# Two phases per weight chunk: the products with its hi part first, then those with its lo part

## The reference

```python
z = rms_norm(h, mix_norm_gain[i]) @ w_in[i]                        # 2048 x 2112
h = h + jnp.concatenate([y_pool, y_mla], axis=-1) @ w_out[i]
q = (xn @ w_pq)                                                    # in peer()
act = jax.nn.gelu(jnp.einsum('tkd,td->tk', expert_u[ib], xb))      # rows gathered by index
return jnp.einsum('tk,tkd->td', act * gb, expert_v[ib])
proj = h @ w_in                                                    # second block, 2048 x 11264
return x + merged @ w_out
```

## Time and profile before

| | |
|---|---|
| median of 3 runs | 2645.71 us (2640.82 to 2649.74) |
| the profiled execution | 2644.75 us, its span 2643.3 us |
| mean granted clock of TensorE | 0.955 of full speed |
| busy, share of the span | PE 80%, DVE 54%, ACT 24%, POOL 25% |
| products | 7418 instructions on PE |
| HBM read | 747.84 MB, of which 207.63 MB over the queue of SP and its like, the rest gathered rows |

### The profile page before, as it was taken

How to read it: one execution, slowest core, us unless ns; L and a number is a source line. 1 busy time by engine, 2 the same in 40 slices (tenths; PEclk the granted TensorE clock), 3 DMA queues, 4 the chain that set the end, 5 groups by cost and what they waited for, 6 DMA issues and landing times.

```text
span 2643.3 us, 18981 instructions
## 1 busy us (share of the span) xinstructions
PE 2125.3 (80%) x7418; PEld 1361.2 (51%) x7418; DVE 1432.7 (54%) x1772; ACT 645.3 (24%) x857; POOL 648.1 (25%) x522
## 2 busy tenths in 40 slices
PE   7988887444777777777777777777999999999998
PEld 6876666331222222222222222224778778788887
DVE  4456457777667644444444444454554565654453
ACT  4244342121000000000000000012443353543342
POOL 0000001324554554445444554440000000000000
PEclk9988888767999999999999999999999999999999
DMA  5433246667999999999999999995545544455554
GB/s 215 158 119 117 86 177 222 240 237 311 422 421 421 422 421 422 422 422 421 422 422 421 422 421 422 421 422 225 175 161 194 204 141 154 173 176 191 191 188 146
DMA packets 104488, 751.19 MB, mean 284 GB/s; under 512 B 11856, under 2 KB 11856, under 8 KB 13264
## 3 DMA queue, kind: packets, MB, share of 16 engines
q0 software_dynamic: 73728, 536.90, 49.3%
q1 hardware_dynamic: 28512, 207.63, 22.4%
q10 hardware_dynamic: 2160, 5.45, 0.5%
HBM read 747.84 MB, written 2.10 MB: 284 GB/s over the span
## 4 chain that ended last, share of the span: by engine, by line
PE 44%; DMA 35%; DVE 12%; ACT 4%; issue 3%; POOL 2%; ACTq 0%; SPq 0%; POOLq 0%; DVEq 0%
DMA xT_rows<-in_expert_v,idx 26%; PE ps L278 11%; PE ps L279 11%; PE ps L280 11%; PE ps L512 8%; DMA W<-in_expert_u,idx 6%; DVE wlo L1038 3%; DMA xT_rows<-in_expert_u,idx 2%; DVE W L1339 2%; ACT whi L667 2%; POOL W L243 1%; POOL xT_rows L243 1%; PE ps L305 1%; DMA W<-in_expert_v,idx 1%; DVE W L1423 1%
## 5 line engine op out<-in xcount | busy, mean ns | idle before, releaser
L1038 DVE TENSOR_TENSOR wlo<-raw,whi 128x2048 fp32r<-128x2048 f32 x195 | 446.1, 2290 | 369.4 <-ACT whi L667 369.3
L278 PE MATMUL ps<-whi,xT 128*128 128x512 f32 (+1 forms) x1432 | 575.7, 402 | 85.8 <-DVE wlo L1038 82.9
L512 PE MATMUL ps<-xT_rows,W 128*128 128x512 f32 x960 | 448.0, 609 | 205.6 <-DMA xT_rows<-in_expert_v,idx 200.3
L279 PE MATMUL ps<-wlo,xT 128*128 128x512 f32 (+1 forms) x1432 | 568.2, 397 | 0.0
L280 PE MATMUL ps<-whi,xT 128*128 128x512 f32 (+1 forms) x1432 | 566.8, 396 | 0.0
L512 PE MATMUL ps<-W 128*128 128x512 f32 x960 | 442.3, 602 | 152.0 <-DMA W<-in_expert_v,idx 145.6
L667 ACT ACTIVATE whi<-raw 128x2048 fp32r<-128x2048 f32 x195 | 372.6, 1913 | 488.8 <-PE ps L280 470.4
L512 PEld LDWEIGHTS ps<-xT_rows,W 128*128 128x128 f32 x960 | 174.2, 192 | 478.7 <-issue 274.5
L1423 DVE CUSTOM_DVE_ANT_0 W<-W 128x2048 f32<-128x2048 f32 x112 | 256.4, 2292 | 265.2 <-DMA W<-in_expert_u,idx 264.7
L1423 DVE CUSTOM_DVE_ANT_0 xT_rows<-xT_rows,W 128x2048 f32<-128x2048 f32 x112 | 256.4, 2292 | 260.1 <-DMA xT_rows<-in_expert_u,idx 259.9
L512 PEld LDWEIGHTS ps<-W 128*128 128x128 f32 x960 | 172.0, 189 | 422.0 <-issue 236.0
(11 more groups left out here) (236 smaller groups left out, 1152.9 us busy)
## 6 DMA issues: line engine op xcount, KB each, us to landing
raw<-in_weights SPq DMA_DIRECT2D x196, 1024.0 KB, 4.9
W<-in_expert_u,idx POOLq DMA_INDIRECT x144, 16.4
h<-in_x SPq DMA_DIRECT2D x2, 1024.0 KB, 6.9
xT_rows<-in_expert_v,idx POOLq DMA_INDIRECT x128, 15.8
W<-in_expert_v,idx POOLq DMA_INDIRECT x128, 15.8
out<-h ACTq DMA_DIRECT2D x8, 256.0 KB, 4.7
xT_rows<-in_expert_u,idx POOLq DMA_INDIRECT x112, 16.4
W<-in_pool_op ACTq DMA_DIRECT2D x1, 1024.0 KB, 15.7
```

Of the source, the lines that this page charges most:

```text
L278: pe.matmul(o, a[0], b[0], start=start, stop=False)
L279: pe.matmul(o, a[0], b[1], start=False, stop=False)
L512: m = pe.matmul(ps[:, (4 if t == 0 else 0) + b, :], diag[:, i % DIAGS, :], slots[n % GR][:, b * NC:(b + 1) * NC], start=(unit % NH == 0 an ...
L1038: v.tensor_tensor(lo, raw[:, c % RAW, :], hi.bitcast(F32), ALU.subtract).then_inc(sem["lo_done"], 1)
```

## The change

Each chunk's products are issued in two phases. First the sixteen with the hi part of the weights (x_hi w_hi and x_lo w_hi), after a wait for `hi_done` only; the sixteenth raises a new semaphore, `hi_used`. Then, after a wait for `lo_done`, the eight with the lo part (x_hi w_lo); the last raises `used` as before. ScalarE's split of chunk c waits for `hi_used` of the chunk that was in the same `whi` slot, and for its `lo_done` (VectorE reads `whi` to make the lo part). VectorE's split gets a second wait, `used` of the chunk that was in the same `wlo` slot. `SPLIT_BEFORE[c]` is that chunk: c - 2, except where that would be C_KEYS, whose parts lie elsewhere: for c = 43 it is 39. `HI_USED` turns a chunk's number into the count of `hi_used`, which the four chunks outside `block_step` do not raise; where one of these was in the slot, ScalarE waits for `used` as before. The chunk of the rope columns (64 columns wide, 96 products) is treated in the same way, 64 and 32. The order within the first phase is for each slice and tile hi, then lo part of the activations; the sums in PSUM are made of the same terms in another order.

```diff
+OTHER_CHUNKS = (C_POOL, C_KEYS, C_PROJ, C_PROJ + 1)
+SPLIT_BEFORE = [c - 2 * SPL if c - SPL == C_KEYS else c - SPL for c in range(CHUNKS)]
+HI_USED = [sum(b not in OTHER_CHUNKS for b in range(c + 1)) for c in range(CHUNKS)]
...
-                pe.wait_ge(sem["lo_done"], c + 1)
                 hi, lo = whi[:, c % SPL, :], wlo[:, c % SPL, :]
                 nk = 4 if cols_n == NC else DK
+
+                def product(k, t, x, w_, start, stop):
+                    s = slice(t * 128, (t + 1) * 128)
+                    cs = slice(k * cols_n, (k + 1) * cols_n)
+                    return pe.matmul(ps[:, banks_of(b) + t, 0:cols_n], x[:, q0 + qn * 4 + k, s], w_[:, cs], start=start, stop=stop)
+
+                pe.wait_ge(sem["hi_done"], c + 1)
                 for k in range(nk):
                     for t in range(NT):
-                        s = slice(t * 128, (t + 1) * 128)
-                        cs = slice(k * cols_n, (k + 1) * cols_n)
-                        ks = q0 + qn * 4 + k
-                        m = matmul3(ps[:, banks_of(b) + t, 0:cols_n], (lh[:, ks, s], ll[:, ks, s]), (hi[:, cs], lo[:, cs]),
-                                    start=(qn == 0 and k == 0), stop=(qn == n_q - 1 and k == nk - 1))
+                        product(k, t, lh, hi, qn == 0 and k == 0, False)
+                        m = product(k, t, ll, hi, False, False)
+                m.then_inc(sem["hi_used"], 1)
+                pe.wait_ge(sem["lo_done"], c + 1)
+                for k in range(nk):
+                    for t in range(NT):
+                        m = product(k, t, lh, lo, False, qn == n_q - 1 and k == nk - 1)
                 m.then_inc(sem["used"], 1)
...
             def split(c):
                 a.wait_ge(landed[c % RAW], 16 * (c // RAW + 1))
                 if c >= SPL and c != C_KEYS:
-                    a.wait_ge(sem["used"], c - SPL + 1)
+                    if SPLIT_BEFORE[c] in OTHER_CHUNKS:
+                        a.wait_ge(sem["used"], SPLIT_BEFORE[c] + 1)
+                    else:
+                        a.wait_ge(sem["hi_used"], HI_USED[SPLIT_BEFORE[c]])
+                        a.wait_ge(sem["lo_done"], SPLIT_BEFORE[c] + 1)
                 a.activation(split_into(c)[0], raw[:, c % RAW, :], ACT.Copy).then_inc(sem["hi_done"], 1)
...
             def split(c):
                 hi, lo = split_into(c)
                 v.wait_ge(sem["hi_done"], c + 1)
+                if c >= SPL and c != C_KEYS:
+                    v.wait_ge(sem["used"], SPLIT_BEFORE[c] + 1)
                 v.tensor_tensor(lo, raw[:, c % RAW, :], hi.bitcast(F32), ALU.subtract).then_inc(sem["lo_done"], 1)
```

More of the change, by code:

```diff
@@ L66 @@
 SIGNALS = (
-    "hi_done", "lo_done", "used", "evac0", "evac1", "consts",
+    "hi_done", "lo_done", "hi_used", "used", "evac0", "evac1", "consts",
     "turned", "turned_hi", "turned_lo", "squared", "mean_ok", "root_ok", "rstd_ok", "angle_ok", "sin_ok",
```

## The result

The changed kernel takes 2599.86 us (median of 4 runs, 2595.83 to 2601.45) against 2643.8 for the kernel before in the same comparison (2640.82 to 2649.74): a ratio of 0.983, 95% interval 0.981 to 0.985, so 44 us are saved. Its profiled execution took 2595.83 us, span 2594.4, which is 48.9 less than the span of before. The forecast was 2595, a saving of 49.3 in the profiled execution.

The account below looks back on a forecast made before the run. TensorE's waits for lo parts at both ends, 52.9 us, were taken as the bound that can go; front 24.2 plus end 23.8, plus 1.8, less 0.5, gave 49.3 us: 2644.75 - 49.3 = 2595, range 2582 to 2617.

Parts of the forecast that it names:

- What bounds the kernel: At both ends TensorE works and waits for lo parts, 52.9 us; routing (183 us) and DMA-bound middle (1207 us) cannot shorten.
- the sign: Whole kernel: with equal durations no event comes later, as every new wait is met no later; faster 0.95, slower 0.03.
- The new instructions: TensorE's added wait and increment in the middle of each chunk, 192 times: taken as 0 us.
- The bound of 0.15 us: Upper cost of the mid-chunk wait when only just met: 192 x 0.15 = 29 us, giving 2624; chance 0.03.
- Waits with a late hi part: Chunks such as 3, 0 and 9: the lo-part wait shrinks by 2.3 us each, the hi part becoming late.
- The clock: TensorE's half-speed stretches after waits, at chunks 9, 42 and 45 1.7, 2.5 and 3.0 us, are taken back.
- Rival A: Waits break into shorter ones but slow-clock stretches return all the same: 10 us less gain, 2605; chance 0.18.
- Heads, norms, chunks 42 to 45: Gains at heads (chunks 26 to 28) 4.2 us, norms (chunk 109) nothing, chunk 42 6.7, chunk 45 4.7.
- the correction of 1.8 for modelled ends: Idle times counted from modelled ends of 0.39 us, true step 0.23: 0.16 added for each of 11 waits going whole.
- rival C's small waits: More comes out: uncounted waits, some 0.2 us ahead of a dozen chunks, with start-up and norms: 5 to 10 us, 2588; chance 0.12.
- the middle: Between 430 and 1820 us: early rows with routing (183 us) and DMA-bound stretch (1207 us) stay the same.
- The forecast's last line: A changed middle would show the forecast wrong: weight loads then meet the gathers at other moments; no size given.

Follow-up runs that it names:

- runs 3 and 4: Changed kernel with, respectively, an unused increment on each product of a chunk and an already met wait before each product: 2598.64 us and 2593.43 us.
- run 2: TensorE's two phases alone, ScalarE and VectorE waiting as in the kernel before: 2599.61 us, ratio to the kernel before 0.982.
- run 9: Against the two phases alone (2599.61 us), eight hi-part products first, then the eight lo-part, then the other eight hi-part: 2600.2 us.
- run 8: Nine weight loads of the early-row stretch held for chosen gather landings: 2586.57 us in the changed kernel, 2639.14 us in the kernel before.

## Why the prediction was right

**What bounds the kernel** was right, and with it the sign. TensorE's waits for lo parts at the two ends are gone but for 2 us, and the argument that no event can come later held for TensorE: no chunk starts later than before.

**The new instructions.** 0 us each, from the row across the chunk boundary: right, by a step of 0.23 us in the changed kernel and by runs 3 and 4 with some twenty times as many; the 26 ns an increment of the Trainium skill did not show. The bound of 0.15 us was for a wait only just met, which these runs do not test: at chunks 3, 45, 63 and 79 the first product still starts 0.14 us after the hi part lands, but not at every chunk. For VectorE's added wait the sum had 0.5 us; no run singles it out.

**Waits with a late hi part** (chunks 0, 3, 9, 45, 63, 79, 118): each 2.3 us as worked out, 2.3 to 2.4 measured. **The clock**: taken back whole at chunks 9, 42, 77 and 118, 1.6 + 2.4 + 1.7 + 1.6 us against 1.7 + 2.5 + 1.7 + 1.7. Rival A falls in the places it named. The places are those of one execution: in the second profile of the kernel before, chunk 77 ran at full speed and 63 and 79 did not. What repeats is that between 1820 us and the end the granted clock fell to half three to six times in each of the five traces with the order of before, and not once in six of the seven with the whole change.

**Heads, norms, chunks 42 to 45**: 4.3, 0.0 and 11.2 against 4.2, 0 and 11.4. Asking what is late next, and not how long TensorE idles, gave these: at the norms the idle time would have said 3.9.

**What was mis-sized.** The two ends brought 58.6 us where the sum had 49.3. Of the 9.3 more, 7.7 are at places that the sum left out and 1.0 in the last expert products; the sum's own places brought 49.9, with the correction of 1.8 for modelled ends contained in them. The 7.7 are not all rival C's small waits (5 to 10 us): 3.5 are, and 4.2 lie at chunks 0 and 16 and the softmax, where it was mostly the clock, some 2.5 of them not to be found in most other executions.

**What was wrong: the middle.** The step that took the middle as unchanged ("the same 183 and 1207 us in the middle") failed: the stretch of the early rows took 193.3 us and not 184.2. The expert phase, bound by the DMA engines, did stay (1195.0 and 1195.5). The forecast treated the stretch as VectorE's, since VectorE was busy 139 of 183 us, and did not read the other 44: 40 of them are waits for gathers, and how long these take depends on when ten loads are issued, which the change moves. The forecast's last line named this; it had no price in the sum or in the rivals. The two errors were nearly equal and cancelled, 9.3 against 9.6 (with 0.5 in the expert phase), so that the profiled time came out within a microsecond. That is luck, and so is that the profiled execution was the fastest of the four. The hit is better than the reasoning. That the place of a load has a price was to be read in the trace of before, where one gather takes 6.05 us beside others of 9 to 11; its size, 180 to 193 us for the stretch, took the runs.

**The median** is 4 us above the profiled execution of the changed kernel. Over the traces with the order of before F is 425.0 to 429.4 and E 829.7 to 835.6 us; over the seven with the whole change 400.3 to 405.9 and 800.1 to 803.0. The means are 427.8 and 831.9 against 403.0 and 800.6: 24.8 + 31.3 = 56.1 us for the two ends. Less 9.1 + 0.5 that is 46.5, between the 43.9 of the medians and the 48.9 of the profiled pair.

## What to carry to other kernels

When an operand is made in two steps, order the products so that those which need only the first step come first: that alone was the gain here (run 2), and half of the cover kept most of it (run 9). Size such a change by asking at each wait what is late next, not by the idle time. And where a stretch is not filled by its busiest engine, look at what fills the rest before calling it unchanged: transfers that another engine's progress sets off will meet it at other moments, and tying them to a landing behind which nobody waits (run 8) was worth 13 us.

## What the runs showed of the hardware

A gather of GpSimd issued while VectorE's dot (2.3 us, two operands in SBUF) runs is not through until 0.8 us after the dot: 3.03 us against 0.94, and 0.01 us of timing decided which. A gather of 128 rows of 8 KB took 5.80 us from issue to use with the loads beside it cut to 8 columns, 6.05 with a 1 MB load issued 1.0 us behind it, and 10.78 with one issued 0.4 us behind it and the rest of another still under way; in the 4 us after that issue the loads moved 180 packets and the gathers 14.

Increments on TensorE, and waits that are already met, cost nothing at steps of 0.227 us, 4200 of either.

TensorE's granted clock makes the ends of the kernel vary by 5 us from one execution to the next, in single groups that run at 1.2 instead of 2.4 GHz in one trace and not in another; with the whole change this is left to the first end (400.3 to 405.9 us), while the last took 800.1 or 800.2 in six traces of seven. The same sixteen turns after VectorE's norm, in the changed kernel and with the phases alone:

```profile
2103.51 1.97 PE L316 MATMUL ps<-ident,W 128*128 128x128 f32 x16 [2.15 <-DVE W L1532]
```

```profile
2106.34 3.57 PE L315 MATMUL ps<-ident,W 128*128 128x128 f32 x16 [2.15 <-DVE W L1525]
```

The granted clock over them was 1.00 and 0.52 of full speed. Both follow the same wait of 2.15 us, and the groups and waits ahead of them are the same as well, so what TensorE did before does not tell them apart here; that is left open. A difference of a few microseconds between two traces should be looked for in such groups first.
